# The opening of a fused two-block kernel, normalised by tokens and turned on TensorE

## The reference

```python
silu_c, silu_cc = jax.nn.silu(c), jax.nn.silu(c_ctx)
sh1, sc1, gt1, sh2, sc2, gt2 = jnp.split((silu_c @ w_mod[i] + b_mod[i])[:, None, :], 6, axis=-1)
mod_c = jnp.split(silu_cc @ w_mod[i][:, :n_mod * D] + b_mod[i][:n_mod * D], n_mod)

h     = rmsnorm(x,   g_pre_mix[i]) * (1 + sc1)      + sh1
h_ctx = rmsnorm(ctx, g_pre_mix[i]) * (1 + mod_c[1]) + mod_c[0]
k_a, v_a, k_b, v_b, q_a, q_b, g_a, g_b = split_cols(h @ w_in, IN_SPLITS)
parts = split_cols(h_ctx @ w_in[:, :KV_COLS], IN_SPLITS[:4])
```

## Time and profile before

| | us |
|---|---|
| median of 3 runs | 1773.88 |
| lowest and highest | 1773.38, 1775.60 |
| the profiled execution | 1777.78 |
| its span, first to last instruction | 1776.0 |

### The profile page before, as it was taken

The page is one execution under the profiler, slowest core; times in us unless marked ns, Lnnn a source line. Parts: engine busy times, 40 slices in busy tenths (PEclk is TensorE's granted clock), DMA queues, the critical chain, the costliest instruction groups (busy, mean ns, idle before and its releaser), DMA issues.

```text
span 1776.0 us, 19653 instructions
## 1 busy us (share of the span) xinstructions
PE 1685.5 (95%) x7790; PEld 841.3 (47%) x7791; DVE 464.9 (26%) x1031; ACT 240.9 (14%) x491; POOL 9.0 (1%) x5
## 2 busy tenths in 40 slices
PE   4999999899999999999999999999989999999998
PEld 2766677433333333332333333333344687588853
DVE  2303442421212212121212212121231623144411
ACT  2013440100000000000000000000131321100000
POOL 0010000000000000000000000000000000000000
PEclk9999999899999999999999999999989999999999
DMA  9652845569999999999799999999973232434400
GB/s 394 267 126 99 347 174 201 198 285 417 430 428 429 428 429 428 428 430 428 292 419 428 428 429 428 429 428 428 428 287 142 95 142 68 181 142 161 170 25 24
DMA packets 47841, 530.21 MB, mean 299 GB/s; under 512 B 13780, under 2 KB 13908, under 8 KB 15672
## 3 DMA queue, kind: packets, MB, share of 16 engines
q1 hardware_dynamic: 36720, 522.21, 71.0%
q10 hardware_dynamic: 11080, 7.42, 1.6%
HBM read 528.55 MB, written 1.06 MB: 298 GB/s over the span
## 4 chain that ended last, share of the span: by engine, by line
PE 71%; DMA 24%; DVE 3%; ACT 1%; issue 1%; SPq 0%; ACTq 0%; DVEq 0%
DMA ring<-experts_dram 23%; PE scores L1839 17%; PE proj L1551 10%; PE proj L2085 9%; PE att_out L1876 7%; PE proj L1541 6%; PE proj L2097 4%; PE proj L1668 3%; PE proj L1717 3%; PE turned L1807 2%; PE scores L1826 1%; PE scores L1633 1%; PE att_out L1657 1%; DMA rows<-rows_dram 1%; PE proj L1587 1%
## 5 line engine op out<-in xcount | busy, mean ns | idle before, releaser
L1839 PE MATMUL scores<-ring,arena 128*64 128x512 f32 x2112 | 472.1, 594 | 23.1 <-DMA ring<-experts_dram 19.8
L1839 PEld LDWEIGHTS scores<-ring,arena 128*64 128x64 f32 x2112 | 148.9, 137 | 333.1 <-issue 273.0
L1876 PE MATMUL att_out<-ring,arena 128*64 128x512 f32 x1024 | 233.9, 598 | 0.0
L1551 PE MATMUL proj<-ring,arena 128*128 128x512 f32 x384 | 170.1, 601 | 3.1 <-DVE arena L1116 2.5
L2085 PE MATMUL proj<-arena,ring 128*128 128x256 f32 x704 | 153.6, 382 | 0.7 <-ACT arena L813 0.7
L1290 DVE COPY arena<-turned 128x512 f32<-128x512 f32 x33 | 22.8, 692 | 480.4 <-PE turned L1807 480.4
L2085 PEld LDWEIGHTS proj<-arena,ring 128*128 128x128 f32 x704 | 134.7, 192 | 19.4 <-ACT arena L813 0.9
L1876 PEld LDWEIGHTS att_out<-ring,arena 128*64 128x64 f32 x1024 | 68.0, 136 | 140.9 <-issue 140.9
L1551 PEld LDWEIGHTS proj<-ring,arena 128*128 128x128 f32 x384 | 73.0, 192 | 92.1 <-issue 88.0
L1541 PE MATMUL proj<-arena,ring 128*128 128x256 f32 x512 | 113.1, 381 | 0.0
L1541 PEld LDWEIGHTS proj<-arena,ring 128*128 128x128 f32 x512 | 96.5, 190 | 14.9 <-issue 1.8
(11 more groups left out here) (318 smaller groups left out, 1127.6 us busy)
## 6 DMA issues: line engine op xcount, KB each, us to landing
ring<-experts_dram SPq DMA_DIRECT2D x190, 2048.0 KB, 21.8
ring<-stream_dram SPq DMA_DIRECT2D x54, 2048.0 KB, 8.9
arena<-experts_dram SPq DMA_DIRECT2D x2, 2048.0 KB, 9.9
ring<-stream_dram SPq DMA_DIRECT2D x2, 1024.0 KB, 17.9
arena<-rpb_dram ACTq DMA_DIRECT2D x16, 128.0 KB, 4.3
arena<-gain_rows_dram ACTq DMA_DIRECT2D x3, 512.0 KB, 5.4
arena<-xT_dram SPq DMA_DIRECT2D x1, 1024.0 KB, 7.4
arena<-ctxT_dram SPq DMA_DIRECT2D x1, 1024.0 KB, 9.7
```

What stands on the lines that cost most here:

```text
L1551: ins = mm(pb[:, 0:n], src[:, k, tt * P:tt * P + P], W[:, k, 0:n], start=k == 0, stop=k == KD - 1)
L1839: ins = mm(AS[n][parts, :], xe[:, k % 4, k // 4, :], W[:, kk, n * D + feats.start:n * D + feats.stop], start=False, stop=k == KD - 1, skip ...
L1876: ins = mm(AO[parts, :], act_s[:, kk, s - 4, :], W[:, kk, feats], start=s == 4 and kk == 0, stop=s == 5 and kk == 3)
```

## The change

The input layout changes: `xT` and `ctxT` are gone, `xtok` is loaded first, and the context comes by tokens (`ctxtok`).

- **Norms by tokens.** With tokens on the partitions ACT sums the squares of each token itself while it squares (`token_squares`, with an accumulating output), so that the 16 matmuls with ones are gone. DVE multiplies by the reciprocal root of each token (`normed_tokens`). PE turns the normed tiles, 16 of x and 16 of the context, four to a bank of PSUM, ahead of `mod_part`; ACT copies the turned x to `sqx`, DVE the turned context to `sqc`.
- **Constants.** ACT first loads `cols` and then 130 columns of `cst` (identity, eps, one). The other 1569 columns, `rows` and the router's weights are issued after `hT` is complete, under a semaphore of their own (`later_consts_in`). The router's weights are laid out anew in memory, with each partition's data in one piece. A table load for the root is called ahead, right behind the tanh.
- **First projection.** PE waits for the k-tiles of `hT` (and `hcT`) one at a time rather than for all eight.

```diff
-            sp.dma_start(xT, A["xT"]).then_inc(x_in, 16)
-            sp.dma_start(ctxT, A["ctxT"]).then_inc(ctx_in, 16)
+            sp.dma_start(xtok[:], A["xtok"]).then_inc(x_in, 16)
+            sp.dma_start(ctok, A["ctxtok"]).then_inc(ctx_in, 16)
             for n in range(N1):
                 load(n)
-                if n == RING - 1:
-                    sp.dma_start(xtok[:], A["xtok"]).then_inc(xtok_in, 16)
...
-            act.dma_start(cst[:], A["cst"]).then_inc(consts_in, 16)
             act.dma_start(cols[:], A["cols"]).then_inc(consts_in, 16)
-            act.dma_start(rows[:], A["rows"].partition_broadcast(P)).then_inc(consts_in, 16)
-            act.dma_start(wr[:], A["w_router"].rearrange("(k p) n -> p k n", p=P)).then_inc(router_in, 16)
-            act.wait_ge(consts_in, 48)
+            act.dma_start(cst[:, 0:CONST_EARLY], A["cst"][:, 0:CONST_EARLY]).then_inc(consts_in, 16)
+            act.wait_ge(consts_in, 32)
...
+            nc.scalar.activation(dummy, C("one"), ACT.Sqrt)
+            def token_squares(src, n):
+                for tt in range(TT):
+                    nc.scalar.activation(spare_start[:, tt, :], src[:, tt, :], ACT.Square, scale=D ** -0.5,
+                                         accum_out=start_ms[:, 2 * n + tt:2 * n + tt + 1]).then_inc(sq_ready, 1)
+                act.wait_ge(sq_ready, 2 * n + 2)
+                nc.scalar.activation(start_r[:, 2 * n:2 * n + 2], start_ms[:, 2 * n:2 * n + 2], ACT.Sqrt,
+                                     bias=C("eps")).then_inc(root_ready, 1)
...
+            for b in range(4):
+                act.wait_ge(xn_turned, b + 1)
+                nc.scalar.activation(sqx[:, 2 * b:2 * b + 2, :],
+                                     [PB[2], PB[3], PT, AO][b][:, :].rearrange("p (a t) -> p a t", t=T), ACT.Copy)\
+                  .then_inc(scaled_ready, 1)
...
             act.wait_ge(h_ready, KD)
+            act.dma_start(cst[:, CONST_EARLY:], A["cst"][:, CONST_EARLY:]).then_inc(later_in, 16)
+            act.dma_start(rows[:], A["rows"].partition_broadcast(P)).then_inc(later_in, 16)
+            act.dma_start(wr[:], A["w_router"]).then_inc(router_in, 16)
             act.dma_start(modbg, A["mod_bias_gain"]).then_inc(modbg_in, 16)
...
+            for n, (src, banks) in enumerate(((xnorm, (PB[2], PB[3], PT, AO)), (ctok, (AS[0], AS[1], PB[2], PB[3])))):
+                pe.wait_ge(xn_ready, 2 * n + 2)
+                for b in range(4):
+                    if n == 1 and b >= 2:
+                        pe.wait_ge(scaled_ready, b - 1)
...
-            pe.wait_ge(h_ready, KD)
+            pe.wait_ge(ctx_scaled, 4)
             need(4)
-            for src in (hT, hcT):
-                if src is hcT:
-                    pe.wait_ge(hc_ready, KD)
+            for src, made in ((hT, h_ready), (hcT, hc_ready)):
                 pb = bank()
                 for tt in range(TT):
                     for k in range(KD):
+                        if tt == 0:
+                            pe.wait_ge(made, k + 1)
                         ins = mm(pb[:, tt * 256:tt * 256 + 256], src[:, k, tt * P:tt * P + P],
```

More of the change, by code:

```diff
@@ L63 @@
 CONST, CONST_N = layout([
-    ("ident", P), ("ones", P), ("tri", TT * T), ("causal", P), ("gla_mask", CHUNK), ("window", GRID_W),
-    ("iota", P), ("cos", TT * DH), ("sin", TT * DH), ("carry", T), ("before32", NE), ("turn_id", 1), ("eps", 1),
-    ("one", 1),
+    ("ident", P), ("eps", 1), ("one", 1), ("ones", P), ("tri", TT * T), ("causal", P), ("gla_mask", CHUNK), ("window", GRID_W),
+    ("iota", P), ("cos", TT * DH), ("sin", TT * DH), ("carry", T), ("before32", NE), ("turn_id", 1),
 ])
+CONST_EARLY = P + 2
 COLS, COLS_N = layout([
@@ L212, in two_blocks @@
         Va = region(11264, 4, 512)
-        ctxT = region(11264, KD, T)
+        ctok = region(11264, TT, D)
         sqc = region(13312, KD, T)
+        spare_start = region(4096, 2, D)
         qb = region(13312, TT, 512)
@@ L314, in two_blocks @@
         ge2 = region(9728, 2, 2, T)
-        rstd = tiny(T)
-        rstd_c = tiny(T)
+        start_ms = tiny(4)
+        start_r = tiny(4)
         cs = tiny(32 * KD).rearrange("p (k c) -> p k c", c=32)
@@ L362, in two_blocks @@
         sq_ready = sem("squares_ready")
-        sum_ready = sem("sum_of_squares_ready")
+        later_in = sem("later_consts_in")
+        xn_ready = sem("normed_tokens_ready")
+        xn_turned = sem("normed_tokens_turned")
+        ctx_scaled = sem("context_turned_copied")
         root_ready = sem("root_ready")
@@ L595, in step @@
                 act.wait_ge(act_step, n_step[0])
-            act.dma_start(cst[:], A["cst"]).then_inc(consts_in, 16)
             act.dma_start(cols[:], A["cols"]).then_inc(consts_in, 16)
-            act.dma_start(rows[:], A["rows"].partition_broadcast(P)).then_inc(consts_in, 16)
-            act.dma_start(wr[:], A["w_router"].rearrange("(k p) n -> p k n", p=P)).then_inc(router_in, 16)
-            act.wait_ge(consts_in, 48)
+            act.dma_start(cst[:, 0:CONST_EARLY], A["cst"][:, 0:CONST_EARLY]).then_inc(consts_in, 16)
+            act.wait_ge(consts_in, 32)
             cc = col("c", 0, 2 * KD).rearrange("p (k c) -> p k c", c=2)
             nc.scalar.activation(cse, cc, ACT.Tanh, scale=0.5).then_inc(cs_exp, 1)
[L608 to L614, removed]
+            nc.scalar.activation(dummy, C("one"), ACT.Sqrt)
[6 more added lines that the diff above has]
+                                     bias=C("eps")).then_inc(root_ready, 1)
             act.wait_ge(x_in, 16)
-            squares(xT, sqx)
+            token_squares(xtok, 0)
             act.wait_ge(ctx_in, 16)
-            squares(ctxT, sqc)
-            root(1, AS[0], rstd)
-            root(2, AS[1], rstd_c)
+            token_squares(ctok, 1)
+            for b in range(4):
[3 more added lines that the diff above has]
+                  .then_inc(scaled_ready, 1)
             bank = [0]
@@ L960, in bc, with normed_tokens @@
                     ap.unsqueeze(2).to_broadcast([P, ap.shape[-1], n])
[L962 to L966, removed]
+            def normed_tokens(src, dst, n):
+                dve.wait_ge(root_ready, n + 1)
+                step(V.reciprocal(start_r[:, 2 * n:2 * n + 2], start_r[:, 2 * n:2 * n + 2]))
+                for tt in range(TT):
+                    V.tensor_scalar(dst[:, tt, :], src[:, tt, :], start_r[:, 2 * n + tt:2 * n + tt + 1], None,
+                                    ALU.mult).then_inc(xn_ready, 1)
             cc = col("c", 0, 2 * KD).rearrange("p (k c) -> p k c", c=2)
             step(V.memset(cs, 0.0))
-            dve.wait_ge(consts_in, 48)
+            dve.wait_ge(consts_in, 32)
             dve.wait_ge(cs_exp, 1)
@@ L975, in _ @@
             dve.wait_ge(x_in, 16)
-            scale_rows(xT, sqx, 1, rstd).then_inc(scaled_ready, 1)
+            normed_tokens(xtok, xnorm, 0)
             dve.wait_ge(ctx_in, 16)
-            scale_rows(ctxT, sqc, 2, rstd_c).then_inc(scaled_ready, 1)
+            normed_tokens(ctok, ctok, 1)
+            for b in range(4):
+                dve.wait_ge(xn_turned, 4 + b + 1)
+                V.tensor_copy(sqc[:, 2 * b:2 * b + 2, :],
+                              [AS[0], AS[1], PB[2], PB[3]][b][:, :].rearrange("p (a t) -> p a t", t=T))\
+                 .then_inc(ctx_scaled, 1)
+            dve.wait_ge(ctx_scaled, 4)
             def modulation(g, T_bank):
@@ L1062, in _ @@
             step(ins)
+            dve.wait_ge(later_in, 32)
             V.tensor_tensor(q3, q3, bc(row("g_q"), 16), ALU.mult)
@@ L1501, in _ @@
             mm = nc.tensor.matmul
[L1503 to L1513, removed]
+            pe.wait_ge(consts_in, 32)
+            for n, (src, banks) in enumerate(((xnorm, (PB[2], PB[3], PT, AO)), (ctok, (AS[0], AS[1], PB[2], PB[3])))):
+                pe.wait_ge(xn_ready, 2 * n + 2)
+                for b in range(4):
+                    if n == 1 and b >= 2:
+                        pe.wait_ge(scaled_ready, b - 1)
+                    for c in range(2):
+                        for tt in range(TT):
+                            ins = nc.tensor.transpose(banks[b][:, c * T + tt * P:c * T + tt * P + P],
+                                                      src[:, tt, (2 * b + c) * P:(2 * b + c) * P + P], ident)
+                    ins.then_inc(xn_turned, 1)
             B = [0]
@@ L2099, in _ @@
                 ins.then_inc(down_done, 1)
-INPUTS = ["w_router", "b_gu", "b_dn"]
+INPUTS = ["b_gu", "b_dn"]
 def slots(w, cols):
@@ L2162 @@
     arrays["experts"] = np.concatenate([gu, dn], axis=1)
-    arrays["xT"] = features_first(get("x")[0])
+    arrays["w_router"] = np.ascontiguousarray(get("w_router")[0].reshape(KD, P, NE).transpose(1, 0, 2))
     arrays["xtok"] = np.ascontiguousarray(get("x")[0].reshape(TT, P, D).transpose(1, 0, 2))
@@ L2171 @@
     arrays["gain_rows"] = np.stack([get("norm_mix_g_2")[0], get("norm_ffn_g_2")[0], get("norm_final_g_2")])
-    arrays["ctxT"] = features_first(get("ctx")[0])
```

(1 more changed line is left out.)

9 lines of the change are left out of this document (4 added, 5 removed).

## The result

| | before | after |
|---|---|---|
| median, us | 1773.88 (5 runs) | 1763.61 (5 runs) |
| lowest and highest | 1772.73, 1777.96 | 1763.08, 1766.62 |
| profiled execution and its span | 1777.78, 1776.0 | 1765.16, 1763.3 |

The ratio is 0.9938, 95% interval 0.9922 to 0.9953: 10.3 us or 0.6% faster, well clear of noise. Five more runs of the same kernel on another occasion had a median of 1766.11 (1764.14 to 1766.71) against 1774.92, ratio 0.9943 (0.9929 to 0.9956). So the median moves by 2.5 us between occasions. That the forecast of 1763.6 met the first of them to a hundredth is chance. Both medians lie within the forecast range.

What follows compares the result with a forecast made beforehand. PE (71% of the chain) bounds the kernel, its opening late through constants and sums. Weights' chain 5.5, pacing 3.1 and clock 1.7 give a 10.3 us shift: 1773.9 to 1763.6 us, range 1760.5 to 1768.4.

Steps and rivals of the forecast that it cites:

- Bound and first term: Modulation matmuls: slot 3 is the next late transfer, landing at 28.9 us; they end at 30.7 against 36.16, 5.5 earlier.
- Hidden turns: PE before slot 3 lands: turns and three quarters of the modulation are done before 28.9 us, hidden under the weights' transfer.
- Pacing and clock: First projection: waiting by k-tile gains 3.1 us and a clock still high 1.7 us; it ends at 47.3.
- Later constants at no cost: Late `cst` and `rows`, issued from 36.5 us: `rows` lands at 52, DVE reads at about 68, so no cost.
- The shift reaches the end: Whole kernel: the first projection's 10.3 us earlier end counts in full, with the first expert chain piece near 572 us.
- such stretches in one direction: Rival (6%): slot 3 lands nearer 27.5 and a cold stretch elsewhere, seen at 335 to 340, shortens by 1.7; 1760.5 us.
- cold rival: Last slot and first projection: clock at half after PE idles; projection ends at 50.4, shift 7.2, total 1766.7 us; chance 22%.

Runs made afterwards that it cites:

- constants ahead: Changed kernel with late constants, gains and router weights issued again at the head of ACT's queue, nothing newly waiting for them; 1769.06 us, ratio 0.9963 to before.
- pacing alone: Kernel before with only the first projection's wait by single k-tiles added; 1771.92 us, ratio 0.9985 to before.
- by features: Kernel before with k-tile pacing and late constants, without norms by tokens and turns; 1765.29 us, ratio 0.9949 to before.
- without pacing: Changed kernel, but the first projection waits for all eight k-tiles of hT again; 1770.27 us, ratio 0.9971 to before.
- constants were awaited: Changed kernel with late transfers back at the head of ACT's queue and ACT waiting for late constants and gains before its first operation; 1778.31 us, ratio 1.0019.

## Why the prediction was right, and where not

**Bound and first term.** Right. Slot 3 took the place of the constants as the last to arrive. It landed at 28.13 where I had 28.9, and the modulation ended at 30.15, forecast 30.7. The size was a little small: 4.0 us earlier than before, not 3.2. Landings differ by up to 0.6 us between traces, so no more can be made of that. The experiment with the constants ahead agrees, 3.6 us for the 2.9 that bandwidth alone gives.

**Hidden turns.** Right, with 21.15 for "at 21" and 1.68 us to spare. What I had not seen, and could have worked out from the same rows, is that the old way would have been hidden as well. With constants at 8.8 rather than 17.2 the sums of squares end at 21.2 too. I took the parts of the diff as one and asked only whether the new order is in time. By the runs, 57.61 to 47.17 divides into pacing 4.65, late constants 5.73 and norms by tokens 0.06 us, each from one trace without a cold last quarter. The last of them is nothing within what two traces differ by.

**Pacing and clock.** Right for the kernel with pacing alone and for the first trace: alone they gave 4.65, forecast 4.8 as the sum of 3.1 and 1.7, and the clock stood at 1.00. The idle time that I compared was not of one kind: the 4.6 us of before count from the turn's end, my 2.4 from the modulation's. Counted from the turn the new gap was 1.29. In the second trace the pacing held and the 1.7 us of clock did not come: the projection took 15.74 us.

**Later constants at no cost.** Right: no wait on DVE, landing 14 us ahead.

**The shift reaches the end.** Right, and the trace overstates it. The spans differ by 12.7 us, 2.3 more than the opening. The first two expert loads in the chain, and the long stretch of the second block, after:

```profile
541.20 24.09 DMA ring<-experts_dram
...
569.16 25.49 DMA ring<-experts_dram
...
1526.39 155.24 PE proj L2101 x704
```

The load at 569.16 answers to the one at 582.94 and is 13.8 us early. The chain has one load more ahead of it, at 541.20, since PE, now further ahead of the experts' weights, already waits for that one, by 0.17 us. So PE meets the transfer of the weights one expert sooner, at next to no cost. Of the 3.3 us beyond the opening's, 3.2 came in one place, the first expert's work. The windows show why, first before and then after (PEclk is the third number from the end):

```profile
366.00:368.00 2.00, 2.00 (x5) 0.50 (x4) 0.76 (x2) 0.00 (x0) 0.00 (x0) 0.50 0.99 426
```

```profile
354.00:356.00 2.00, 2.00 (x6) 0.61 (x4) 1.93 (x4) 0.00 (x0) 0.00 (x0) 1.00 1.09 459
```

The clock stood at 0.50 there before, from 366 to 372, and did not fall after. The stretch at 1526 in turn is 1.6 us longer than in the trace before, with a longer low clock at its start. Whether the fall at the first expert's work belongs to the change is not shown. Of the fourteen traces six have it: the kernel before, pacing alone, by features, without pacing, and both with the constants ahead. The other eight, both of the changed kernel among them, don't. It isn't the opening's length that decides, for the kernel by features had the short opening and the fall. The medians of the first occasion differ by 10.3 us, those of the second by 8.8. I had allowed 1.7 us for such stretches in one direction; they moved by 3.2 and by 1.6.

**The chances.** I gave the cold rival 22%. Of three traces of the kernel's own opening up to slot 3 (two of the kernel, one without pacing), two were cold. Three traces are few, but they put it nearer to even odds than to 22%, and a median somewhere between 1763.6 and 1766.7 is all that could be forecast. What I used against it, that the clock of before fell only 4.2 us after PE's last work, was too weak: in the three cold traces it fell between 2.2 and 2.8 us after PE's last work.

## What to carry to other kernels

When a wait is taken off the head of a chain, look for the transfer that is next, and price the change by that alone. Then ask of each part of the change whether the old way would be in time against the new bound; here two small edits made the gain, and the largest none. Put the small transfers that everything waits for ahead of the large ones, on the same queue: here that brought them in at 3.4 us instead of 8.8 or 11.3. An engine paced by transfers can be hurt by being ready earlier: here the clock fell in the three traces with a gap of 2.9 us or more ahead of the last slot, and in none where it was 1.8 or less. And don't take two traces' difference for the effect of an edit before looking at what came ahead of it: a transfer that lands late behind the edit may have been late ahead of it.

## What the runs showed of the hardware

Turns raise TensorE's pace. In the kernel with turns made twice PE did nothing else from 14.94 to 24.75, and by the starts in its timeline sixteen records took 3.43 us at first (14.94 to 18.37) and 1.75 later (21.16 to 22.91). In the kernel whose constants were awaited the turns began only at 29.34. Their first eight records took 1.74 us from start to start, the last eight 0.96 (33.69 to 34.65), so it is not the time since the kernel's start that counts. The Trainium skill, page "TensorE: Matmul & The Clock Gate", Part 4, says that a turn does not count as activity in this way; these fp32 turns did. The granted clock in the records was 1.00 throughout, so at the start of a kernel it says nothing, and durations have to.

A small transfer landed later beside larger ones. 65 KB of constants took 7.6 us to land beside 1 MB transfers, 10.2 us beside 2 MB ones, and 2.2 us ahead of both on one queue. The last of them also changed queues, so the place in the order and the queue were not separated.
